# Hybrid decoder block on 8 cores: rows of the second conv half and four weight blocks are requested behind the last selection mask

## The reference, cut to what matters

```python
h = rms_norm(x, norm_mix)
z = h @ w_in                                   # q, three pairs of k and v, gates, u
o_cmp, p_cmp = compressed_attention(q, k_cmp, v_cmp, slopes)
sel_idx = select_blocks(p_cmp, T)              # top 16 of 32 blocks, per query
o_slc = selected_attention(q, ksl, vsl, sel_idx, slopes)
o_win = window_attention(q, kw, vw, slopes)
o_nsa = g0 * o_cmp + g1 * o_slc + g2 * o_win
# conv group: a * sigmoid(b), depthwise causal conv of width 31, layer norm, silu
o_conv = silu(layer_norm(conv(a * sigmoid(b)) + conv_b))
x = x + concat([o_nsa, o_conv]) @ w_out
```

## Time and profile before

| | |
|---|---|
| median of three runs | 1772.19 us (1771.73 to 1772.25) |
| the profiled execution's own time | 1772.91 us |
| its span on the slowest core, core 4 | 1771.7 us |
| spans of the eight cores | 1752.9 to 1771.7 us |
| PE busy on core 4 | 1629.3 us, 92% |
| mean granted clock of TensorE, core 4 | 0.974 |

### The profile page before, as it was taken

The page is one execution under the profiler, slowest core; times in us unless marked ns, Lnnn a source line. Parts: engine busy times, 40 slices in busy tenths (PEclk is TensorE's granted clock), DMA queues, the critical chain, the costliest instruction groups (busy, mean ns, idle before and its releaser), DMA issues.

```text
span 1771.7 us, 29703 instructions; the slowest of 8 cores (1752.9 to 1771.7 us)
## 1 busy us (share of the span) xinstructions
PE 1629.3 (92%) x10362; PEld 905.3 (51%) x10530; DVE 1025.9 (58%) x1948; ACT 557.3 (31%) x965; POOL 99.2 (6%) x158
## 2 busy tenths in 40 slices
PE   4899999999998388997689899999999999999998
PEld 2566555667664246865344344444444444444443
DVE  3554122575755454433554767777777776767776
ACT  2453244778788373233451010100101010010100
POOL 0000000000004200000000000000000000000000
PEclk9899999999999699998899999999999999999999
DMA  9953444226028538238205173533535435263514
GB/s 215 256 159 59 88 89 92 58 47 122 3 55 168 97 92 189 69 72 143 47 10 110 26 143 72 95 72 72 96 67 104 90 74 95 48 119 72 96 24 190
DMA packets 40688, 168.12 MB, mean 95 GB/s; under 512 B 6240, under 2 KB 22240, under 8 KB 22368
## 3 DMA queue, kind: packets, MB, share of 16 engines
q0 software_dynamic: 17904, 113.42, 35.8%
q1 hardware_dynamic: 22640, 52.79, 10.1%
HBM read 262.24 MB, written 8.52 MB: 153 GB/s over the span
## 4 chain that ended last, share of the span: by engine, by line
PE 85%; DMA 4%; DVE 3%; ACT 3%; issue 2%; SPq 2%; POOL 1%; DVEq 0%; ACTq 0%; POOLq 0%
PE pair L1589 15%; PE bank L1589 12%; PE bank L1641 9%; PE pair L1641 9%; PE bank L538 5%; PE pair L538 4%; PE pair L1027 4%; PE bank L766 3%; PE bank L761 3%; PE bank L1337 3%; PE bank L1006 3%; SPq L313 2%; DMA arena<-xc 2%; PE pair L1397 2%; PE pair L545 2%
## 5 line engine op out<-in xcount | busy, mean ns | idle before, releaser
L1589 PE MATMUL pair<-arena 128*128 128x512 bf16 x1251 | 287.1, 379 | 1.4
L1016 ACT ACTIVATE arena<-bank,arena 128x512 bf16<-128x512 f32 (+3 forms) x402 | 213.6, 588 | 83.2 <-PE bank L1006 31.4
L1589 PE MATMUL bank<-arena 128*128 128x512 bf16 x948 | 219.1, 379 | 0.7
L1589 PEld LDWEIGHTS pair<-arena 128*128 128x128 bf16 x1280 | 125.3, 98 | 151.0
L1608 ACT COPY arena<-pair 128x512 f32<-128x512 f32 x40 | 23.4, 586 | 515.0 <-PE pair L1589 503.5
L1641 PE MATMUL bank<-arena 128*128 128x512 bf16 x686 | 166.1, 381 | 7.8 <-DVE arena L1644 5.6
L1641 PE MATMUL pair<-arena 128*128 128x512 bf16 x690 | 165.1, 379 | 0.8
L1027 PE MATMUL pair<-arena 128*128 128x129 bf16 (+1 forms) x1184 | 124.0, 226 | 31.8 <-DVE arena L1020 30.4
L1589 PEld LDWEIGHTS bank<-arena 128*128 128x128 bf16 x960 | 93.9, 98 | 113.3
L1644 DVE TENSOR_TENSOR arena<-bank,arena 128x512 f32<-128x512 f32 x176 | 121.7, 692 | 31.2 <-PE bank L1641 31.2
L1644 DVE TENSOR_TENSOR arena<-pair,arena 128x512 f32<-128x512 f32 x176 | 121.7, 692 | 29.8 <-PE pair L1641 29.8
(11 more groups left out here) (200 smaller groups left out, 1989.2 us busy)
## 6 DMA issues: line engine op xcount, KB each, us to landing
arena<-wblk POOLq DMA_DIRECT2D x108, 1024.0 KB, 9.8
arena<-xc SPq DMA_DIRECT2D x24, 1024.0 KB, 12.7
arena<-arena SPq DMA_DIRECT2D x64, 135.0 KB, 2.7
y<-arena SPq DMA_DIRECT2D x8, 1024.0 KB, 4.0
arena<-sel SPq DMA_DIRECT2D x28, 256.0 KB, 6.6
arena<-memb SPq DMA_DIRECT2D x2, 1024.0 KB, 10.2
arena<-cbf SPq DMA_DIRECT2D x1, 360.2 KB, 24.7
arena<-biasT SPq DMA_DIRECT2D x1, 153.0 KB, 2.1
```

Source lines behind the costliest of these rows:

```text
L1016: op(ACT, lambda: nc.scalar.activation(out=Pt[pj][:, c:e], in_=bank[si][:, c:e], func=AF.Exp, bias=biasT[:, bc:bc + 1]), r=[bankb[si], bia ...
L1589: op(PE, lambda: nc.tensor.matmul(bank[bi][:, :], lhsT=lhs[:, k, :], rhs=rhs[:, k, :], start=(fresh and k == 0), stop=(k == 7), skip_group ...
```

## The change

Three edits. After `conv_half(0)` the limit of the weight queue is no longer raised. In `conv_half` tiles are requested up to a limit that is 8 at first, so rows for k = 8 to 12 are not requested there. Both are caught up in `spread` of the last pass, n = 3, behind the mask's loads and behind the triangle's product.

```diff
             yield from conv_half(0)
-            wissue(len(self.wq))
-
-        h4_free, h4_at, h4_next = [], {}, [0]
+
+        h4_free, h4_at, h4_next, h4_last = [], {}, [0], [8]
...
                 h4_free.append(h4_at.pop(k))
-                h4_more(16)
+                h4_more(h4_last[0])
...
                     op(POOL, lambda: nc.gpsimd.tensor_tensor(out=blk, in0=blk, in1=tri01, op=ALU.mult), r=[cbb], w=[Emdb[m]])
+                if n == 3:
+                    h4_last[0] = 16
+                    if h4_next[0] >= 8:
+                        h4_more(16)
+                    wissue(len(self.wq))
             when([selbfb], spread)
```

## The result

Before: 1771.99 us median (1771.73 to 1772.25). Changed: 1753.43 us median of four runs, of which three took 1751.94, 1753.06 and 1753.81 us; the fourth, in which one die had a lower clock, took 1796.94 us and counts in that median but not in the ratios. The ratio is 0.9892, with an interval of 0.9873 to 0.9912: 1.1% faster, some 19 us. The forecast was 1750.8, with a range of 1745 to 1759.

What follows compares the result with a forecast made beforehand. The bound was the last pass's late mask, sharing transfers with four weight blocks. Subtractions 24.4 us earlier less 3.0 lost gives 21.4 off 1772.9, 1751.5; the runs' median lies 0.7 lower: 1750.8 us, range 1745 to 1759.

Steps and rivals of the forecast that it cites:

- The mask's lateness: Last attention pass: mask took 40.6 us from store to triangle, against 14.5 in pass 1, because four weight blocks share transfers.
- rival "no change": Mask slow through gathers in flight on SP or its parts' own pattern, not the weights; time stays 1772 us; chance 0.03.
- The times on SP and POOL: Around the last pass's mask: store about 558.97 us, triangle 573.5 instead of 600.1, subtractions from 577.2, 24.4 us earlier.
- The backlog of 6.9 MB: Gathers and weights moved behind the mask land at 615.6 us, 9 us before attention ends; costed at nothing.
- The slower rival: Moved gathers and weights end so late that residual rows and output projection start late; 1784 us at 75 GB/s; chance 0.03.
- The subtractions: POOL's eight, beside attention: 11.69 us, slowing DVE's masked products to 1.48 us; five products to catch up, 3.0 us lost.
- A rule weighed: Skill page's 358 GB/s would land the mask in 5.9 us, triangle near 568, total near 1748.4 us; measured 165 GB/s preferred.
- Core 4 should stay the slowest: Whole kernel: the other late cores have the same hole as core 4, and early cores such as core 2 gain less.
- the wait for `xc` within 5 us of 7.1: Expected sign before the output projection: DVE's wait for the residual rows stays within 5 us of its 7.1 us.
- The sum for core 4's span: Mask landing to end of attention: subtractions 24.4 us earlier less 3.0 for catching up gives a gain of 21.4 us.
- rival "less is gained": The moved 6.9 MB land slower than 164 GB/s and run into conv or residual rows; 1755 to 1765 us; chance 0.17.
- Core 4's rest of the span: End of attention to end of span, 1125.9 us before; growth by more than 5 us would show the prediction wrong.

Runs made afterwards that it cites:

- Weights alone: Changed kernel, but only the four weight requests move behind the triangle's product; gathers of k = 8 to 12 stay ahead of the mask's store: 0.9907 of the kernel before.
- gathers alone: Changed kernel, but only the gathers move behind the mask; the four weight blocks are requested at the end of the first conv half as before: 1.0005.
- two blocks: Changed kernel, but two of the four weight blocks are requested at the end of the first conv half again, beside the mask: 0.9939 of the kernel before.

## Why the prediction was right, and where it was off

**The mask's lateness: right, and shown.** Weights alone bring 0.9907 beside the change's 0.9892, with overlapping intervals; gathers alone bring nothing, two blocks half. The rival "no change", by which SP is held by its gathers or the parts by their own pattern, fell with the same runs: the issues' 29.35 us were the weights' doing.

**The times on SP and POOL: right.** Store 558.97 forecast, 557.97 measured; mask issues 5 to 7, 5.46; triangle 573.5, 572.86; subtractions from 577.2, 577.17; SP's first gather behind attention 624.4, 623.66; the residual request 632.5, 632.88. The gain of core 4's span was put at 21.4 and was 21.1.

**The backlog of 6.9 MB costs nothing: right for its own landing.** At 605 to 615 us the transfers carry 15 GB/s on core 4, and on core 6 they carry 5, and 2 from 615 to 625. The slower rival needed the backlog to last until 653.9.

**The subtractions: the sum nearly right, its mechanism mis-sized.** The prediction had DVE catch up in products of 1.48 us each, for 3.0 us lost. Instead one product was held 8.28 us and PE stood 9.8 us. The forecast end of attention still came out, within a microsecond: from the triangle to SP's first gather it was 45.7 us before, the prediction added 2.2 and 3.0 to it, and it is 50.8. Only the sum was right, and as the mechanism was another, that is luck. Part of what made up for the hold is on DVE itself: on core 4 its masked products take 93.1 us in all (88.4 before) and its norm products 11.0 (14.1 before), since in the old order of events POOL slowed three norm products that it now leaves alone. How the rest cancelled is not shown. What the whole meeting costs now is 10 to 11 us, by the run without the subtractions and by the run with them on DVE. The Trainium skill, page "SBUF — State Buffer", section "Who interferes with whom", has an instruction of DVE with two inputs in SBUF and one of POOL that reads SBUF share ports under a lock, and says: "Issue order, not op shape, decides who blocks." The runs agree that shape does not decide (a 128x4 operation was held as long as a 128x512 one), and with the requests behind the subtractions the turns of 1.2 us fit an instruction's length. That the order decides they do not bear out, as far as the booked starts tell: DVE was held whether it started 0.09 us ahead of the chain or 0.6 us behind. And with the requests directly ahead one instruction was held for about seven of POOL's, of which the page tells nothing.

**The page's figure in "A rule weighed".** By the prediction's own numbers 5.9 us in place of 12.7 puts the triangle at 566.7 us and not near 568, and how 1748.4 us follows is not shown. Nothing else hangs on it, and the triangle at 572.86 bears out the slower rate.

**"Core 4 should stay the slowest": wrong.** It is core 6, and in the two other executions core 2 and core 3, so the slowest core is not fixed by the program. Core 6's mask hole closed in the same way (DVE's wait for `sel` of 23.2 us is gone), but it gained only 16.2 us, while its wait for `xc` grew from 7.9 us to 16.2. Waits of core 6 from 640 to 760 us in the kernel before:

```profile
DVE arena L1340 <- DMA arena<-xc: 7.9, 1, 7.9
```

The same in the changed kernel:

```profile
DVE arena L1344 <- DMA arena<-xc: 16.2, 2, 9.1
```

The step that failed is "the wait for `xc` within 5 us of 7.1": 15.4 us on core 4 and 16.2 on core 6, two waits each. The sum for core 4's span gave 1750.3, and it was 1750.6; core 6's 1752.6 is 2.0 us above that, most of the 2.6 us by which the median of 1753.43 missed. By its size it belongs to the rival "less is gained", but not by its cause. That rival had the moved 6.9 MB run into the residual rows. On core 4 those had landed by 605 to 615 us, at least 17 us before the residual rows were asked for at 632.88; what shares with the residual rows is the next weight blocks, which are asked for at 635.87 and 645.38 on core 6. The run that defers these takes the wait to zero on every core.

**Core 4's rest of the span.** From SP's first gather behind attention to the end it was 1125.9 us and is 1750.6 - 623.66 = 1126.9, so of core 4's longer `xc` wait hardly anything shows in its end. The projection's matmuls show where it went on each core (start of the first and of the last, us, before and changed):

```
        first            last
core 4  668.6 -> 646.2   816.4 -> 796.6
core 6  669.2 -> 646.9   814.0 -> 799.0
```

Both cores enter the projection 22.3 to 22.4 us earlier. Core 6 leaves it 15.0 us earlier: it lost 7.3 us inside. Core 4 leaves it 19.8 us earlier and lost 2.6; it had been longer in the projection before (147.8 us, core 6 144.8), so it had less to lose. The projection takes 139.0 us where no core waits for `xc`. Measured by that, core 4 lost 8.8 us in it before and 11.4 now, and core 6 lost 5.8 and 13.1. Over the eight cores it starts 19.2 us earlier in the mean and ends 14.5 us earlier, so about a quarter of the gain up to its start is lost inside it. Why core 4 lost more than core 6 before, with a wait no longer, is open.

**Open.** Why the wait for `xc` is long on some cores and short on others (5.3 to 8.4 us), and on others again in the next run. That the cores are now more in step and ask at the same time is an argument, not a result: no run here set the cores apart, and the same edit helped the kernel before, too. Open too is why requests for weights directly ahead of POOL's chain make it run without giving way.

## What to carry to other kernels

When a small load that everyone waits for is slow, look at what another queue asked for within a microsecond of it: long issues on its own queue can be the effect, and bulk with a later use belongs behind the load's landing. Closing one hole brings the next shared transfer nearer, so look for the next place where late data and prefetch meet, and make the prefetch wait there too. And a chain of elementwise work on POOL beside a busy DVE is paid by DVE: here it was cheaper to give DVE the work.

## What the runs showed of the hardware

- A DVE operation on 128x4 f32, 1.08 us on core 4 in the change, was held 8.71 us beside a chain of eight POOL operations (9.80 us), and a 128x512 bf16 product 8.28 us, when POOL's four DMA requests stood right ahead of the chain. In six kernels with two or four requests right ahead, on eight cores each, one DVE instruction was held 8.05 to 9.25 us every time. With the requests behind the chain the two engines took turns, and on eight cores no DVE instruction took over 1.75 us.
- The eight issues of the mask on SP took 5.46 or 5.79 us with no weights in flight, 16.88 us with two 1 MB weight loads on the other queue and 29.70 us with four, for the same instructions.
- From the mask's store to its landing it took 14.8 us with none of these loads beside it, 28.9 with two and 40.1 with four, in the mean of eight cores.
- Eight POOL subtractions of 128x512 f32 beside DVE's masked products cost 10 to 11 us of the kernel's time; on DVE they delayed the output projection by some 1.5 us.
